# Two transformer blocks on one core: waits per PSUM bank, gate tiles of the Hyena projections last, rotation by a shuffle, and key sums in four column groups

## The reference, cut to what matters

```python
for layer in range(2):                       # second_block
    h = modulate(rms_norm_2(x, norm_mix[layer]), shift1, scale1)
    q, k, v, hy, g = split(h @ w_in[layer], PROJ_SPLITS)
    q = apply_rope(split_heads_norm(q, q_norm[layer], 8), cos, sin)
    k = apply_rope(split_heads_norm(k, k_norm[layer], 2), cos, sin)
    attn = latent_attention(q, k, v, kc, vc)
    hyo = hyena_mix(hy, conv_w, conv_b, *filt, hyena_bias)
    x = x + gate1 * (sigmoid(g_a) * (attn @ w_o_attn) + sigmoid(g_h) * (hyo @ w_o_hyena)) @ w_out
    x = x + gate2 * swiglu_2(modulate(rms_norm_2(x, norm_ffn[layer]), shift2, scale2), w_gate_up, w_down)

def hyena_mix(u, ...):
    x0, x1, v = split(short_conv(u, conv_w, conv_b), 3)    # 3 x 512 channels
    v = v * x1
    y = bidirectional_long_conv(v, h_fwd, h_bwd) + v * bias
    return y * x0                                          # x0 is the gate
def apply_rope(t, cos, sin):        # pairs (t0, t1) of neighbouring channels
    return stack([t0 * cos - t1 * sin, t0 * sin + t1 * cos])
```

## Time and profile before

| | |
|---|---|
| median of 3 runs | 2011.11 us (2008.76 to 2011.85) |
| the profiled execution's own time | 2010.59 us |
| its span, first to last instruction | 2008.8 us |
| busy: PE, DVE, ACT, POOL | 1908.4, 966.6, 754.1, 108.6 us |
| mean granted TensorE clock | 0.978 |

### The profile page before, as it was taken

How to read it: one execution, slowest core, us unless ns; L and a number is a source line. 1 busy time by engine, 2 the same in 40 slices (tenths; PEclk the granted TensorE clock), 3 DMA queues, 4 the chain that set the end, 5 groups by cost and what they waited for, 6 DMA issues and landing times.

```text
span 2008.8 us, 29272 instructions
## 1 busy us (share of the span) xinstructions
PE 1908.4 (95%) x12348; PEld 1652.5 (82%) x12348; DVE 966.6 (48%) x1125; ACT 754.1 (38%) x916; POOL 108.6 (5%) x106
## 2 busy tenths in 40 slices
PE   7999998999998999999999899999989989989998
PEld 6989895898986887767887788887867767989997
DVE  5545465554655436663324422223344575564454
ACT  5334434433445433163223422222234435343333
POOL 3000201200004100000000100000010010000000
PEclk9999998999999999899999999999989999999999
DMA  9996385599541422002233233322234211546641
GB/s 256 323 301 244 126 305 215 180 327 277 184 169 65 141 84 84 0 1 73 95 105 84 81 88 104 90 98 103 86 109 136 84 43 63 180 135 189 182 174 63
DMA packets 288760, 283.55 MB, mean 141 GB/s; under 512 B 8760, under 2 KB 265669, under 8 KB 282515
## 3 DMA queue, kind: packets, MB, share of 16 engines
q1 hardware_dynamic: 287312, 279.56, 43.9%
q0 software_dynamic: 1120, 2.46, 0.4%
q10 hardware_dynamic: 227, 0.06, 0.0%
HBM read 280.84 MB, written 1.07 MB: 140 GB/s over the span
## 4 chain that ended last, share of the span: by engine, by line
PE 85%; DVE 5%; ACT 4%; POOL 2%; issue 1%; DMA 1%; ACTq 0%; SPq 0%; DVEq 0%
PE PS L1583 25%; PE PS L1584 24%; PE PS L1585 24%; PE PS L1694 2%; PE PS L2135 1%; POOL X L579 1%; PE PS L2085 1%; PE PS L2123 1%; POOL SQ L563 1%; PE PS L2098 1%; DVE WLO L1007 1%; ACT PB L916 1%; PE PS L1983 1%; PE PS L2157 1%; ACT WHI L624 1%
## 5 line engine op out<-in xcount | busy, mean ns | idle before, releaser
L1583 PE MATMUL PS<-AHI,WHI 128*128 128x256 f32 (+1 forms) x2480 | 795.2, 321 | 24.6 <-DVE ALO L1308 7.1
L1584 PE MATMUL PS<-ALO,WHI 128*128 128x256 f32 (+1 forms) x2480 | 784.9, 317 | 0.0
L1585 PE MATMUL PS<-AHI,WLO 128*128 128x256 f32 (+1 forms) x2480 | 784.5, 316 | 0.0
L1007 DVE TENSOR_TENSOR WLO<-RAW,WHI 128x2048 fp32r<-128x2048 f32 x210 | 485.1, 2311 | 437.8 <-ACT WHI L624 437.7
L1583 PEld LDWEIGHTS PS<-AHI,WHI 128*128 128x128 f32 x2480 | 477.6, 193 | 87.7 <-issue 28.3
L624 ACT ACTIVATE WHI<-RAW 128x2048 fp32r<-128x2048 f32 x210 | 400.4, 1908 | 286.2 <-PE PS L1585 266.1
L1584 PEld LDWEIGHTS PS<-ALO,WHI 128*128 128x128 f32 x2480 | 477.9, 193 | 29.7 <-issue 1.2
L1585 PEld LDWEIGHTS PS<-AHI,WLO 128*128 128x128 f32 x2480 | 477.6, 193 | 28.8
L1583 PE MATMUL PS<-SHI,WHI 128*128 128x256 f32 (+1 forms) x704 | 219.9, 312 | 2.3 <-DVE HB L1560 2.3
L1584 PE MATMUL PS<-SLO,WHI 128*128 128x256 f32 (+1 forms) x704 | 217.9, 310 | 0.0
L1585 PE MATMUL PS<-SHI,WLO 128*128 128x256 f32 (+1 forms) x704 | 217.9, 309 | 0.0
(11 more groups left out here) (257 smaller groups left out, 1702.3 us busy)
## 6 DMA issues: line engine op xcount, KB each, us to landing
RAW<-in_w_in_dram SPq DMA_DIRECT2D x98, 512.0 KB, 4.5
MRAW<-in_w_mod_dram SPq DMA_DIRECT2D x48, 1024.0 KB, 6.7
RAW<-in_ffn_w_gu_dram SPq DMA_DIRECT2D x88, 512.0 KB, 7.5
RAW<-in_w_gate_up_dram SPq DMA_DIRECT2D x88, 512.0 KB, 4.9
...
```

The lines of the kernel that those rows point to most:

```text
L1007: dve.tensor_tensor(WLO[:, c % RING, :], RAW[:, c % RING, :], WHI[:, c % RING, :].bitcast(F32), ALU.subtract)\
L1583: pe.matmul(out, whi, xhi, start=first, stop=False, skip_group_check=shared)
L1584: pe.matmul(out, whi, xlo, start=False, stop=False, skip_group_check=shared)
L1585: return pe.matmul(out, wlo, xhi, start=False, stop=last, skip_group_check=shared)
```

## The change

In the stages of the second block alone, for both layers:

- The six Hyena chunks are loaded and multiplied in another order (HY_ORDER): x1, v, and the gate x0 last. turned(0) stands between the two tiles of chunk 5, its copy VTT ahead of that chunk's eviction, and forward() waits only for the taps of the chunks whose banks it overwrites.
- The rotation leaves PE: DVE swaps neighbouring partitions with stream_shuffle into BR, multiplies BR by a sine table that carries the sign, and adds. POOL's cosine product stays. ROT and its load go.
- The keys' sums go into bank 6 in four column groups of 32 partitions (8 products of 128 columns), root and reciprocal are over 256 columns instead of 1024, and key_rows() spreads the rows back over all partitions with 8 products, which stand between the two tiles of the next chunk. In layer 0 the sums stand behind chunk 0, in layer 1 behind chunk 1 (KEYS_AT); the queries' sums and rotations follow from two chunks later on.
- The copy VT2 (in a new place of SBUF) comes before the HHI split, and HLO behind normalise2(0) and maxima(1).
- mix starts when the first half of the oh result is copied, out starts when the sigmoids have left its bank, and down starts with banks that gate_up doesn't hold and waits for the others one by one.

```diff
+SWAP = [p ^ 1 for p in range(32)]
+HY_ORDER = (2, 3, 4, 5, 0, 1)
+KEYS_AT = (0, 1)
...
-                    if q == 1:
+                    if q == KEYS_AT[layer]:
                         act.wait_ge(S("qkv_ev"), 6 * layer + 6)
                         act.activation(HSQ[:, :, :], QKV[:, 8:10, :], ACT.Square).then_inc(S("h_sq"), 1)
-                    if q >= 3:
-                        query_pair(q - 3)
+                    if q >= KEYS_AT[layer] + 2:
+                        query_pair(q - KEYS_AT[layer] - 2)
...
+                    if q == 5:
+                        act.wait_ge(S("y_tr"), 2 * layer + 1)
+                        act.activation(VTT[:, :, :], PS[:, 0:2, :], ACT.Copy).then_inc(S("y_vt"), 1)
                     act.wait_ge(S("pe_done"), c + 1)
                     for t in range(2):
-                        m = 2 * q + t
+                        m = 2 * HY_ORDER[q] + t
                         act.activation(HY[:, m, 0:nt], ring2(q, nt)[:, t, :], ACT.Identity,
...
-                        act.activation(HSQ[:, :, :], PS[:, 6:8, :], ACT.Sqrt, scale=1.0 / DH2, bias=EPSC[:, 0:1])\
+                        act.activation(HSQ[:, 0, 0:TX], PS[:, 6, 0:TX], ACT.Sqrt, scale=1.0 / DH2, bias=EPSC[:, 0:1])\
...
                 exps(0)
+                act.wait_ge(S("v_tr"), layer + 1)
+                act.activation(VT2[:, :, :], PS[:, 4:6, :].rearrange("p a (b n) -> p (a b) n", n=P), ACT.Copy)\
+                   .then_inc(S("v_ev"), 1)
                 act.wait_ge(S("y_h"), y_done)
                 for m in range(HT):
                     act.activation(HHI[:, m, 0:nt], HY[:, 8 + m, 0:nt], ACT.Copy).then_inc(S("hh_hi"), 1)
-                act.wait_ge(S("hh_lo"), HT * (layer + 1))
-                act.wait_ge(S("v_tr"), layer + 1)
-                act.activation(VT2[:, :, :], PS[:, 4:6, :].rearrange("p a (b n) -> p (a b) n", n=P), ACT.Copy)\
-                   .then_inc(S("v_ev"), 1)
 
                 for u, (grp, h) in enumerate(units):
                     if u + 1 < len(units):
                         exps(u + 1)
                     kts = 4 if grp == 0 else 2
+                    if u == 0:
+                        act.wait_ge(S("hh_lo"), HT * (layer + 1))
...
                 def keys():
 
                     dve.wait_ge(S("h_std"), 2 * layer + 1)
+                    dve.reciprocal(HSQ[:, 0, 0:TX], HSQ[:, 0, 0:TX]).then_inc(S("h_kr"), 1)
+                    dve.wait_ge(S("h_krow"), layer + 1)
                     for kv in range(2):
-                        dve.reciprocal(HSQ[:, kv, :], HSQ[:, kv, :]).then_inc(S("h_kr"), 1)
-                    for kv in range(2):
-                        dve.wait_ge(S("h_kr"), 2 * layer + kv + 1)
                         dve.scalar_tensor_tensor(out=QKV[:, 8 + kv, :], in0=QKV[:, 8 + kv, :], scalar=par("k_norm_2", layer),
-                                                 in1=HSQ[:, kv, :], op0=ALU.mult, op1=ALU.mult).then_inc(S("h_kn"), 1)
-                def rotated(r, tile):
-                    if r:
+                                                 in1=PS[:, 6 + kv, :], op0=ALU.mult, op1=ALU.mult).then_inc(S("h_kn"), 1)
+                def rotated(r):
+                    tile = (8, 0, 2, 4, 6)[r]
+                    if r == 0:
+                        dve.wait_ge(S("h_kn"), 2 * layer + 2)
+                    else:
+                        dve.wait_ge(S("h_gain"), 4 * layer + r)
                         dve.wait_ge(S("h_sum"), 5 * layer + r)
+                    dve.stream_shuffle(BR[:, :, :], QKV[:, tile:tile + 2, 0:TX], SWAP).then_inc(S("h_rot"), 1)
                     dve.wait_ge(S("h_rot"), 5 * layer + r + 1)
-                    dve.tensor_tensor(BR[:, :, :], PS[:, 7, :].rearrange("p (t n) -> p t n", t=2), over_tiles(ROPE[:, 1, :], 2),
-                                      ALU.mult).then_inc(S("h_sin"), 1)
+                    dve.tensor_tensor(BR[:, :, :], BR[:, :, :], over_tiles(ROPE[:, 1, :], 2), ALU.mult).then_inc(S("h_sin"), 1)
...
-                    if q == 2:
+                    if q == KEYS_AT[layer] + 1:
                         keys()
-                    if q >= 4:
-                        rotated(q - 4, (8, 0)[q - 4])
+                    if q >= KEYS_AT[layer] + 2:
+                        rotated(q - KEYS_AT[layer] - 2)
...
-                rotated(2, 2)
-                rotated(3, 4)
-                rotated(4, 6)
+                for r in range(4 - KEYS_AT[layer], 5):
+                    rotated(r)
...
-                for m in range(HT):
-                    dve.wait_ge(S("hh_hi"), HT * layer + m + 1)
-                    dve.tensor_tensor(HLO[:, m, 0:nt], HY[:, 8 + m, 0:nt], HHI[:, m, 0:nt].bitcast(F32), ALU.subtract)\
-                       .then_inc(S("hh_lo"), 1)
                 for u in range(len(units)):
                     normalise2(u)
                     if u + 1 < len(units):
                         maxima(u + 1)
                     if u:
                         attended(u - 1)
+                        continue
+                    for m in range(HT):
+                        dve.wait_ge(S("hh_hi"), HT * layer + m + 1)
+                        dve.tensor_tensor(HLO[:, m, 0:nt], HY[:, 8 + m, 0:nt], HHI[:, m, 0:nt].bitcast(F32), ALU.subtract)\
+                           .then_inc(S("hh_lo"), 1)
...
+                    begin = inst >= 2 and i is None and j == 0
+                    order = ((6, 7, 2, 3, 4, 5, 0, 1) if n == TB else (2, 3, 6, 7, 4, 5, 0, 1)) if begin else range(KT)
+                    for m in order:
+                        if begin and (m if n == TB else m // 2) in (0, 2, 4) and (n == TB or m % 2 == 0):
+                            pe.wait_ge(S("h"), FT * (inst + 1) - ((0, 0, 2, 0, 1)[m] if n == TB else (0, 0, 0, 0, 2)[m]))
...
                     pe.wait_ge(S("h_sq"), 5 * layer + 1)
-                    pe.wait_ge(S("f_fix"), 2 * layer + 2)
+                    if layer == 0:
+                        pe.wait_ge(S("s_ev"), 5)
+                    else:
+                        pe.wait_ge(S("f_fix"), 4)
                     for kv in range(2):
-                        last = pe.matmul(PS[:, 6 + kv, :], ONES[:, :], HSQ[:, kv, :], start=True, stop=True)
+                        for t in range(4):
+                            last = pe.matmul(PS[32 * t:32 * t + 32, 6, kv * P:kv * P + P], ONES[:, 0:32], HSQ[:, kv, t * P:t * P + P],
+                                             start=True, stop=True)
                     last.then_inc(S("h_ss"), 1)
+                def key_rows():
+                    pe.wait_ge(S("h_kr"), layer + 1)
+                    for kv in range(2):
+                        for t in range(4):
+                            last = pe.matmul(PS[:, 6 + kv, t * P:t * P + P], IDENT[:, 32 * t:32 * t + 1].broadcast_to([P, P]),
+                                             HSQ[:, 0, kv * P:kv * P + P], start=True, stop=True)
+                    last.then_inc(S("h_krow"), 1)
...
+                def turned(grp):
+                    if grp == 0:
+                        pe.wait_ge(S("hy_v"), HT * (layer + 1))
+                        pe.wait_ge(S("hy_taps"), 24 * layer + 16)
...
+                for q in range(6):
+                    if q < RING:
+                        pe.wait_ge(S("qkv_ev"), 6 * layer + q + RING + 1)
+                    else:
+                        pe.wait_ge(S("hy_taps"), 24 * layer + 4 * (q - RING + 1))
+                    out = ring2(q, nt)
+                    by_columns(None, FIRST[f"hy{layer}"] + q, [out[:, 0, :], out[:, 1, :]], AHI2, ALO2, nt,
+                               between=(lambda last: turned(0)) if q == 5 else
+                               (lambda last: key_rows()) if q == KEYS_AT[layer] + 1 else None)
+                    if q == 0 and layer == 1:
+                        spectrum(1)
+                    if q == KEYS_AT[layer]:
+                        key_sums()
+                    if q >= KEYS_AT[layer] + 2:
+                        query_sums(q - KEYS_AT[layer] - 2)
...
-                    if y >= 2:
+                    if y >= 4 * layer + 2:
                         pe.wait_ge(S("y_mul"), 7 * (y - 1))
+                    else:
+                        pe.wait_ge(S("hy_taps"), 24 * layer + 20 + 4 * h)
...
-                turned(0)
                 forward(0)
+                if layer == 1:
+                    query_sums(3)
...
-                                pe.wait_ge(S("oh_ev"), 2 * (layer + 1))
+                                pe.wait_ge(S("oh_ev"), 2 * layer + 1)
                             if g == 2:
+                                pe.wait_ge(S("oh_ev"), 2 * layer + 2)
...
-                pe.wait_ge(S("merge"), 12 * (layer + 1))
                 for j in range(4):
-                    if j >= RING:
+                    if j < 2:
+                        pe.wait_ge(S("gate"), 8 * layer + 7 + j)
+                    elif j == 2:
+                        pe.wait_ge(S("merge"), 12 * layer + 11)
...
```

(50 more changed lines are left out.)

27 lines of the change are left out of this document (5 added, 22 removed).

## The result

The changed kernel takes 1988.5 us (median of 4, 1985.57 to 1991.28) against 2011.48 us for the kernel before (median of 4): the ratio is 0.9886, with a 95% interval of 0.9865 to 0.9907. That is 23.0 us less; 19.1 were forecast. The profiled execution took 1991.1 us, 19.5 less than the 2010.6 against which the sum was made. The four executions lie in two pairs, 1985.6 and 1985.9 at a mean granted clock of 0.982, 1991.1 and 1991.3 at 0.976 and 0.977. The profiled one belongs to the longer pair: it lies 2.6 us over its median and the profiled one of the kernel before 0.9 under its own, which makes the distance between 19.5 and 23.0.

What follows compares the result with a forecast made beforehand. PE was taken to bound the kernel, busy 1908.4 of 2008.8 us. The terms 9.6 + 3.5 + 6.5 - 0.5 = 19.1 us, taken from 2010.6, gave 1991.5 us, with a range of 1983 to 2003.

Steps and rivals of the forecast that it cites:

- The border waits: At the starts of mix, out and down: PE's three idle times there count in full, 9.6 us less.
- VT2: Attention of both layers: the earlier copy starts unit 0's transposes sooner, HLO takes some back; 3.5 us less.
- 3.2 at the transposes are 2.1 at PT2: Layer 0's attention: transposes start 3.2 us earlier, but the first PT2 waits for HLO, leaving 2.1 us.
- Layer 0's keys: Layer 0's Hyena stage: spectra(0) starts 7.9 us earlier despite a new stall at key_rows; 6.5 us less counted.
- the fall of 3.4 us: Behind layer 0's stall at key_rows: the clock runs at half speed for 3.4 us, costing 1.7 us.
- the fall in the tail: Layer 0, where PE idles 2.7 us until spectra(0) ends: a clock fall there costs 1.7 us, counted as 1.4.
- Layer 1's keys: Layer 1's Hyena stage: a 5.3 us stall at key_rows and DVE's queue without slack eat PE's saving; -0.5 us.
- The rotation: Hyena rotations on DVE: DVE's and POOL's products go one after the other, so one takes 3.3 us, otherwise 2.8.
- Long falls: Rival: 17 us at half clock behind each of the two new stalls, 2004.8 us; chance 0.17.
- DVE not tight: Rival: no serial products in the rotations and no clock falls, 1983.4 us; chance 0.18.
- Border waits come back: Rival: PE meets the same producers one chunk later, half of 9.6 us and VT2 kept, 1998 us; chance 0.08.
- Dear shuffle: Rival: at 3.3 us each, shuffles on the path six times add 15.6 us, giving 2007; chance 0.07.

Runs made afterwards that it cites:

- e1: The kernel before with only the border waits of mix, out and down taken from the change; 2001.18 us, ratio 0.9951.
- e2: The kernel before with only the copy VT2 moved ahead of HHI and the low parts HLO moved behind maxima(1); 2010.64 us, ratio 1.0.
- e3: The changed kernel with the border waits and the VT2 and HLO moves undone; 2008.59 us, ratio 0.9988 to the kernel before.
- e6: The kernel before with the border waits and the VT2 and HLO moves, without the keys' part; 1997.5 us, ratio 0.9934.
- e5: The changed kernel without the VT2 and HLO moves, so border waits and keys' part together; 1995.61 us, ratio 0.9918 to the kernel before.
- e9: The changed kernel itself, unmodified, measured once more; 1988.9 us, ratio 0.9886 to the kernel before.
- e4: The changed kernel with the keys' reciprocal ahead of the split of weights in DVE's queue; 1979.56 us, ratio 0.9839 to the kernel before.
- e10: e4 with key_rows called behind its chunk instead of between the chunk's tiles; 1976.87 us, ratio 0.9833 to the kernel before.
- e11: e4 with layer 1's split of weights of chunk 5 moved behind the attention in DVE's queue; 1974.8 us, ratio 0.9818 to the kernel before.
- e7: The changed kernel with every shuffle done twice, one after the other; 1994.66 us, ratio 0.9909 to the kernel before.
- e8: The changed kernel with the rotations' product by the cosines on DVE in place of POOL; 1986.57 us, ratio 0.9871 to the kernel before.
- e12: The changed kernel with the edits of e10, e8 and e11 together; 1967.59 us, ratio 0.9783 to the kernel before.

## Why the prediction was right

**The border waits, 9.6.** Right: 9.9 by e1 and 9.6 by the stages of the trace. That it fits to the term is partly luck: the four stages with the oh copy and the merge are 8.1 us shorter for rows of 7.3, and the last hidden tile's 2.3 show as 1.5 in the out, gu and dn stages. No wait for weights or split tiles took their place.

**VT2, 3.5.** Right in the mechanism, and a little small. ACT in layer 0, in the kernel before and in the changed one, exps(0) and the first PT2:

```profile
846.65 0.78 ACT L916 ACTIVATE PB<-PS,NM,RC 128x512 f32<-128x512 f32 x1 [1.71 <-PE PS L2098]
...
855.34 1.02 ACT L936 ACTIVATE PT<-PS 128x1024 f32<-128x1024 f32 x1
```

```profile
840.68 0.78 ACT L919 ACTIVATE PB<-PS,NM,RC 128x512 f32<-128x512 f32 x1 [1.71 <-PE PS L2114]
...
847.19 1.02 ACT L940 ACTIVATE PT<-PS 128x1024 f32<-128x1024 f32 x1 [0.38 <-DVE HLO L1498]
```

There are now 6.5 us between them in place of 8.7, so 2.2 (2.1 forecast); in layer 1 5.6 (1630.24 to 1635.87) in place of 7.4 (1644.33 to 1651.74), so 1.8 (1.4), together 3.9. The step "3.2 at the transposes are 2.1 at PT2" is the growth of the wait for PT2, 8.7 to 10.7. e2 has the same 3.9 in its trace and nothing in its median, since more falls of the clock stand in other stages of it. That moving VT2 causes these falls was not shown; e3, which leaves VT2 as it was, has them as well, and what e2 and e3 share is that the border waits are still there. e6 gives 3.4 and e5 6.4, both within their intervals of 3.9.

**Layer 0's keys, 6.5.** Right, with one small size off. The reciprocal's 1.7 (1.73), the stall of 3.6 (3.04), the fall of 3.4 us (3.42), the 68.0 us from the taps of chunk 0 to those of chunk 5 (68.4), the rotation's 3.3 (3.28), PE's idle time ahead of the first inverse transform of 2.7 (2.52), and spectra(0) 7.9 us earlier (7.7 against its stage's start) are all in the trace. For the fall in the tail I counted 1.4 of 1.7; the first trace has none, e9's has it, and it costs 1.7 there. Of the ten profiled executions with the keys' part six have it, so 1.0 would have been the better count. The text said that the trace has no reciprocal of 256 columns. That was a misreading: in the view by line of the kernel before, the norms' L1083 has four of 128x256 at 1.75 us. The bracket gave the same 1.7, but a row was there to be had.

**Layer 1's keys, -0.5.** Right: the stall is 5.05 (5.3), key_rows takes 3.4 us at half speed from its start to the next product (4.1 were counted), spectra(0) comes 0.4 us earlier against its stage (0.15), the exps 0.7 later. That DVE's queue is the path shows in the start of spectra(0), us from the first Hyena product of the layer:

| | before | changed | e4 | e10 | e11 | e7 | e8 | e12 |
|---|---|---|---|---|---|---|---|---|
| layer 0 | 95.1 | 87.4 | 83.6 | 82.5 | 83.6 | 88.2 | 86.9 | 82.0 |
| layer 1 | 69.2 | 68.8 | 62.5 | 61.7 | 60.3 | 72.8 | 66.3 | 56.9 |

What e7 adds to a rotation and e8 takes from it comes out five times in layer 1 and once in layer 0, and the split that e11 moves comes out in full.

**The rotation, 3.3.** Right (3.28). The Trainium skill ("SBUF — State Buffer", "SBUF: two separate sides") has DVE and GpSimd share a pair of ports by an exclusive lock that the instruction which starts first holds to its end. The trace agrees: DVE's product, which began 0.04 us ahead of POOL's, kept its 0.69 us, and POOL's took 1.77 in place of 1.28; in the earlier trace rows, where POOL's began first, it kept its 1.28 and DVE's grew. The two together last 1.81 us, 0.16 less than one strictly after the other. e8, with no product on POOL, has 2.76.

**The rivals.** Long falls: 3.42 and 6.83 us, not 17. DVE not tight: the rotation took 3.3, and e7's doubled shuffles show no slack. Border waits come back: e1. Dear shuffle: it takes 0.73 us, and in e7's trace a second one in each rotation puts spectra(0) 3.9 us later in layer 1 and 0.75 in layer 0, 4.7 in all.

**The distance from 19.1 to 23.0** is open in part. The profiled executions gave 19.5. That this is so near is in part luck: the two "hy" stages gave 11.2 us where 9.5 were forecast, mostly by the fall that the tail of layer 0 didn't have, and 1.8 us were lost in unchanged code ahead of the change. The medians of both series gave 23. Falls of the clock that come in one execution and not in the next are large enough for it (5.4 us between the two pairs), but nothing here predicts in which they come.
